# Attention layer of a four-layer decoder trunk: the last eight query and gate pieces laid evenly over softmax steps 18 to 28, the first output parts over steps 28 to 31

## The reference, cut to what matters

```
x <- x + RMSNorm_post(mixer(RMSNorm_pre(x)))
```

```
z = h @ w_in                    # 1024 -> q (16 heads x 64), k, v (2 heads x 64), g (1024)
q, k = rope(q), rope(k)
scores = q k^T / 8              # blocks of 128 queries against 256 keys
p = softmax over the keys, with one more "sink" term per head
o = p v
out = (o * silu(g)) @ w_out
```

## Time and profile before

| | us |
|---|---|
| median of 3 runs | 2237.68 (2237.27 to 2237.75) |
| the profiled execution | 2237.23 |
| its span, first to last instruction | 2235.3 |
| PE busy | 2197.0 (98%) |
| DVE busy | 1516.0 (68%) |
| ACT busy | 1118.0 (50%) |
| POOL busy | 107.0 (5%) |

### The profile page before, as it was taken

How to read it: one execution, slowest core, us unless ns; L and a number is a source line. 1 busy time by engine, 2 the same in 40 slices (tenths; PEclk the granted TensorE clock), 3 DMA queues, 4 the chain that set the end, 5 groups by cost and what they waited for, 6 DMA issues and landing times.

```text
span 2235.3 us, 40229 instructions
## 1 busy us (share of the span) xinstructions
PE 2197.0 (98%) x16495; PEld 2118.9 (95%) x16495; DVE 1516.0 (68%) x2211; ACT 1118.0 (50%) x1721; POOL 107.0 (5%) x101
## 2 busy tenths in 40 slices
PE   8999999999999999998999999999999999999997
PEld 7999999999999898887999999999999999999997
DVE  5987787787334756667367778368887787876245
ACT  7445555555332535456362476365546555555232
POOL 0000000000000014445000000000000000000000
PEclk9999999999999999999999999999999999999999
DMA  4322223234411431111322111324222222225213
GB/s 145 124 105 95 96 77 106 85 105 167 149 47 57 164 100 39 48 49 39 114 89 76 48 48 48 124 82 150 95 101 91 86 93 98 86 86 218 95 49 114
DMA packets 76535, 211.67 MB, mean 95 GB/s; under 512 B 10920, under 2 KB 31544, under 8 KB 76344
## 3 DMA queue, kind: packets, MB, share of 16 engines
q1 hardware_dynamic: 72944, 204.19, 26.6%
q10 hardware_dynamic: 3408, 4.90, 0.8%
HBM read 154.23 MB, written 51.13 MB: 92 GB/s over the span
## 4 chain that ended last, share of the span: by engine, by line
issue 43%; PE 42%; DVE 5%; POOL 3%; POOLq 2%; DVEq 2%; ACTq 1%; ACT 1%; DMA 0%
PE ps L1007 18%; PE ps L782 13%; PE ps L808 5%; POOL l_sc L763 3%; PE ps L868 2%; POOLq L762 2%; PE ps L951 1%; PE ps L1236 1%; PE ps L1136 1%; ACTq L1790 1%; POOLq L760 0%; PE ps L942 0%; ACTq L1765 0%; DVE l_hs L2619 0%; DVE l_rc L2608 0%
## 5 line engine op out<-in xcount | busy, mean ns | idle before, releaser
L1007 PE MATMUL ps<-l_h_hi,l_op_hi 128*128 128x258 f32 x1344 | 384.5, 286 | 0.7 <-DVEq L2158 0.7
L1007 PE MATMUL ps<-l_h_lo,l_op_hi 128*128 128x258 f32 x1344 | 379.3, 282 | 0.0
L1007 PE MATMUL ps<-l_t_hi,l_op_hi 128*128 128x258 f32 x1008 | 288.0, 286 | 3.2 <-ACT l_partial L1460 1.7
L1007 PE MATMUL ps<-l_t_lo,l_op_hi 128*128 128x258 f32 x1008 | 285.7, 283 | 0.0
L1007 PE MATMUL ps<-l_h_hi,l_pair_lo 128*128 128x258 f32 x1008 | 284.7, 282 | 0.0
L782 PE MATMUL ps<-l_y_lo,w_hi 128*128 128x344 f32 x816 | 260.0, 319 | 0.0
L1007 PEld LDWEIGHTS ps<-l_h_hi,l_op_hi 128*128 128x128 f32 x1344 | 254.3, 189 | 1.8 <-issue 1.1
L1007 PEld LDWEIGHTS ps<-l_h_lo,l_op_hi 128*128 128x128 f32 x1344 | 254.1, 189 | 0.0
L782 PE MATMUL ps<-l_y_hi,w_hi 128*128 128x344 f32 x726 | 232.5, 320 | 0.9 <-DVEq L2633 0.9
L782 PE MATMUL ps<-l_y_hi,w_lo 128*128 128x344 f32 x726 | 231.4, 319 | 0.0
L1846 DVE TENSOR_TENSOR w_lo<-w_raw,w_hi 128x1024 fp32r<-128x1024 f32 x97 | 122.1, 1260 | 147.0 <-ACT w_hi L1269 143.1
(11 more groups left out here) (314 smaller groups left out, 5520.8 us busy)
## 6 DMA issues: line engine op xcount, KB each, us to landing
w_raw<-in_wu SPq DMA_DIRECT2D x97, 512.0 KB, 3.4
l_pair<-in_wu SPq DMA_DIRECT2D x84, 512.0 KB, 3.5
l_vstage<-v_save SPq DMA_DIRECT2D x32, 516.0 KB, 3.9
y_save<-l_vstage SPq DMA_DIRECT2D x30, 516.0 KB, 2.6
l_y<-y_save SPq DMA_DIRECT2D x30, 516.0 KB, 10.6
v_save<-l_late_v SPq DMA_DIRECT2D x24, 516.0 KB, 2.7
x_save<-x SPq DMA_DIRECT2D x9, 1376.0 KB, 5.8
x<-x_save SPq DMA_DIRECT2D x21, 516.0 KB, 6.9
```

The lines of the kernel that those rows point to most:

```text
L1007: mm = nc.tensor.matmul(ps[:, 2 * j + ch, 0:QW], low[:, k, :] if t == 1 else L.op_hi[i][:, k, :], lo[:, k, :] if t == 2 else hi[:, k, :], ...
```

## The change

The table of pieces and the places of the output parts are written anew. Nothing is added or removed: the same 24 matmuls per piece and the same output parts of 3 matmuls per k-step.

```diff
-                       18: ((28, 0, HALF),), 19: ((28, HALF, KT), (29, 0, KT)), 20: ((30, 0, HALF),), 21: ((30, HALF, KT), (31, 0, KT)),
-                       22: ((32, 0, HALF),), 23: ((32, HALF, KT),), 24: ((33, 0, KT), (34, 0, HALF)), 25: ((34, HALF, KT),), 26: ((35, 0, KT),)}
+                       18: ((28, 0, 6),), 19: ((28, 6, KT), (29, 0, HALF)), 20: ((29, HALF, KT), (30, 0, 2)), 21: ((30, 2, KT),),
+                       22: ((31, 0, 6),), 23: ((31, 6, KT), (32, 0, HALF)), 24: ((32, HALF, KT), (33, 0, 2)), 25: ((33, 2, KT),),
+                       26: ((34, 0, 6),), 27: ((34, 6, KT), (35, 0, HALF)), 28: ((35, HALF, KT),)}
...
-                    if i == 27:
+                    if i == 28:
                         pe.wait_ge(w_lo_done, weighed(u + 18))
+                        pe.wait_ge(*L.piece_read.at(35))
+                        pe.wait_ge(*L.Lo.at(19))
+                        out_part(0, 0, range(0, 2))
+                    if i == 29:
+                        out_part(0, 0, range(2, 6))
+                    if i == 30:
                         pe.wait_ge(*L.piece_read.at(36))
-                        pe.wait_ge(*L.Lo.at(19))
-                        out_part(0, 0, range(0, 3))
-                    if i == 28:
-                        out_part(0, 0, range(3, 6))
-                    if i == 29:
                         pe.wait_ge(*L.Lo.at(22))
-                        out_part(0, 1, range(0, 3))
-                    if i == 30:
-                        out_part(0, 1, range(3, 6))
+                        out_part(0, 1, range(0, 4))
+                    if i == 31:
+                        out_part(0, 1, range(4, 6))
```

## The result

| us | before | changed |
|---|---|---|
| median, 22 runs each | 2237.72 (2236.6 to 2240.24) | 2241.95 (2239.67 to 2246.1) |
| ratio, 95% interval | | 1.0019 (1.0013 to 1.0024) |
| span of the profiled execution | 2235.3 | 2239.8 |

The changed kernel is slower by 4.2 us. That it is slower is certain, since the interval lies above 1. Whether it is slower by more than 0.2% is not, since the interval holds that border. Forecast were 2242.5 us and a rise of 4.8. The profiles show one execution each; the 22 executions of the changed kernel differ by 6.4 us.

The account below looks back on a forecast made before the run. PE, busy 98% of the span, was taken to bound the kernel. Waits +3.0, beginnings 0.3 and clock 1.5 made +4.8 us on 2237.23, plus 0.45 for the median: 2242.5 us, range 2237.6 to 2246.2.

Parts of the forecast that it names:

- before `scores(21)`: Steps 18 and 19: PE waits for maxima(20), which DVE begins later, 2.7 us, bounds 1.0 to 3.0.
- before piece 31 and `scores(24)`: Steps 21 and 22: PE waits 5.7 us for DVE's rotation of tile 7, 0.5 of them before piece 31.
- steps 26 and 27: PE has 9 matmuls less before values(26), the chain loses one tanh: waits 2.3 instead of 3.2 us.
- beginnings: On PE, 17 stretches of pieces and outputs become 19, costing 0.3 us.
- clock behind the first gap: Half clock on PE behind the 2.7 us wait before scores(21): 1.5 us, bounds 0 and 2.0.
- clock behind the second gap: Half clock on PE in step 22, behind the wait before scores(24): 2.0 us.
- clock in step 27: The 2.0 us lost to half clock in step 27 go, since 12 matmuls fill it.
- The stall: DVE's second or third rotation operation stretched to about 2 us beside POOL's multiply, which was taken not to move.
- The third rival: Only the gap of step 22 costs clock: +3.3 us, 2241.0 us, chance 0.17.
- The even spread does what its form says: Rival over the changed steps: all waits and the lost clock go, -10.1, 2227.6 us, chance 0.05.
- Further behind: Rival: both DVE stalls at the upper end, sample keys wait for the cache, +7.8, 2245.5 us, chance 0.08.
- DVE gets through in time: Rival in turns 21 and 22: POOL's multiply misses tile 7's rotation, wait 4.0; sum +0.6, 2238.3 us, chance 0.20.

Follow-up runs that it names:

- Experiment 3: Changed kernel without the nine vector operations that rotate query tile 7, waits and signals kept: 2234.78 us, ratio 0.9985 to the kernel before.
- experiment 1: Changed kernel with only its early part (steps 18 to 22); later pieces from step 24 and output parts as before: 2246.93 us, ratio 1.0039 to the kernel before.
- experiment 4: Changed kernel without POOL's last softmax multiply for blocks 19 and 22: 2236.25 us, ratio 0.9994 to the kernel before.
- Experiment 5: Changed kernel plus 16 and 30 unread matmuls in front of scores(21) and scores(24): 2239.21 us, ratio 1.0007 to the kernel before.
- experiments 2 to 6: Number 2, otherwise unnamed: kernel before up to step 25, piece 35 cut over steps 26 and 27, output parts over 28 to 31; 2237.04 us, ratio 0.9996.
- experiment 6: Against the changed kernel: unit 15 ends in step 19 as before, later pieces spread evenly over steps 20 to 27, output parts over 28 to 31; 2238.61 us.
- experiment 7: Against the changed kernel: table with 42 matmuls in step 19, 36 in step 21, fewer in others, piece 35 whole in step 27; 2233.41 us.

## Why the prediction was right

Step by step, as the prediction put them:

| step | forecast | measured |
|---|---|---|
| before `scores(21)` | 2.7 | 2.85 |
| step 20 | 0 | 0 |
| before piece 31 and `scores(24)` | 5.7 | 0.44 + 5.33 = 5.77 |
| steps 26 and 27 | 2.3 | 1.53 + 0.34 = 1.87 |
| before `values(30)` | 0.7 | 0.68 |
| before `turns(31)` | none | 0.54 |
| waits in all, before 8.44 | 11.4 | 11.71 |
| beginnings | 0.3 | none to be seen |
| clock behind the first gap | 1.5 | 1.49 |
| clock behind the second gap | 2.0 | 1.83 |
| clock in step 27 | -2.0 | -2.0 |
| span | +4.8 | +4.5 |

By the border of 2242.2 us that the prediction had drawn, the measured 2241.95 lies on the side of "same", which had 0.41, and not on that of "slower", which had 0.52. The rise is real but a little smaller than the forecast one. That the sum came so near is in part luck: the waits were 0.3 us larger than forecast, and the beginnings and the second fall smaller by 0.3 and 0.2.

*The large terms.* The method was to count both sides of a meeting from one common start, DVE's queue by distances of starts and PE's by matmuls. It gave 5.7 against 5.77. Experiment 3 shows that it is the rotation in turn 22, and experiment 1 that the loss comes from the early steps and not from the late ones.

*The stall.* The size was right (1.7 us, shown by experiment 4), the operation was not: the rows of before let me expect the second or third of the rotation, and it was the first in both places (982.27 and 1003.92). The multiply starts 0.05 us ahead of it each time. The premise that it doesn't move was wrong. It started at 982.77 before and at 982.22 now. By the rows, that is because POOL's small operation ahead of it ran before DVE's weights began (981.13) and not beside them (980.12). The first row is of before, the second of the changed kernel:

```profile
980.48 0.92 POOL L759 TENSOR_TENSOR l_rq<-l_mx 128x4 f32<-128x4 f32 x1 [6.99 <-ACTq L1696]
```

```profile
980.55 0.20 POOL L760 TENSOR_TENSOR l_rq<-l_mx 128x4 f32<-128x4 f32 x1 [6.99 <-ACTq L1698]
```

Both times now the multiply starts 1.09 us behind the start of the weights (981.13 and 1002.78). For the first gap I had counted a stall of 1.4 us instead of 1.66; it was 1.71, so DVE was 0.3 us later than forecast. PE was 0.15 us later as well (at 986.25 instead of 986.1), and the gap came out 0.15 us longer. The rival of a multiply that misses the rotation did not come; where the multiply would have had to start for that, no run tells.

*The clock.* That it falls behind a gap of 2.7 us was a choice between 0 and 2.0. It fell, at 1.49; that the chosen 1.5 met it so closely is luck. Experiment 5 confirms the sum of both. The third rival (only the second gap costs clock, +3.3 us) is refuted for the profiled execution by the window at 990, and the profiles of experiments 1 and 3 show the fall there too (0.64 and 0.58 in the window 990 to 994). For the 22 executions it isn't settled that each had both falls: their mean granted clock lies between 0.994 and 0.997, the three with 0.997 took 2239.9 to 2240.2 us and the two with 0.994 took 2244.0 and 2244.2.

*The late steps.* The 2.3 came out as 1.87. From `values(24)` to `values(26)` are 12.55 us before (1026.30 to 1038.85) and 11.70 now (1031.50 to 1043.20). So the chain became 0.85 us shorter and not 0.37 (the one tanh), and PE's own work fell by 1.20 and not 1.45: the wait is 1.53 and not 2.3. Against that, 0.34 stayed before `scores(29)`, where none was forecast. What else shortened the chain no run tells. The wait before `turns(31)` was missed. `turns(31)` hangs on a chain through `maxima`, `exps` and POOL that ran inside the 2.30 us of before. In the changed kernel that chain is longer, too. Two rows of the changed kernel belong to it, a small operation of POOL in step 31 and, in the second fence, the weights on DVE:

```profile
1065.47 0.91 POOL L760 TENSOR_TENSOR l_rq<-l_mx 128x4 f32<-128x4 f32 x1 [2.34 <-ACTq L1698]
```

```profile
1065.11 1.22 DVE L1848 TENSOR_TENSOR w_lo<-w_raw,w_hi 128x1024 fp32r<-128x1024 f32 x1
```

The operation of 128 x 4 took 0.91 us and ended at 1066.38, with the weights of DVE, which ended at 1066.33. In experiment 1, where step 31 is as before, it took 0.43 us. That the 0.48 us between them make the wait of 0.54 was not shown. The other profiles fit: in experiments 2 to 6 the operation took 0.90 to 0.92 us and `turns(31)` waited 0.53 to 0.55, and before and in experiment 1 it took 0.44 and 0.43 and nothing waited. But the last two also have the 2.30 us before `values(30)`, so that the two causes are not parted.

*The beginnings.* The 0.3 us for two more stretches were not seen. By the table of the change there are even three more, 17 become 20, which would make 0.45. Waits and clock alone give 4.6 us against 4.5 of span, so that nothing is left for them; a beginning of a stretch seems to cost less than the 0.15 us of the earlier trace rows, but no run took it apart.

*The rivals on the other side.* "The even spread does what its form says" is refuted by the result, and experiment 6 shows no gain from it even with unit 15 on time: an even load on PE did not help where its partner's load was uneven. "Further behind" is refuted by the waits: only two of DVE's turns were late by much, and the sample steps had 0.34 us. "DVE gets through in time" is refuted by the 5.33 us before `scores(24)`.

## What to carry to other kernels

Where one engine's list is laid against a second engine's, don't spread the work evenly but put the most of it beside the second engine's long turns: here the table with 42 and 36 matmuls beside the rotations was 8.5 us faster than the even one, with waits of 2.0 instead of 8.6 us in these steps. When a table moves the end of a unit by one step, count what hangs on that end (readout, weights, rotation) from a common start to its reader, on both engines; that gave the largest term within 0.1 us. And price a gap on the matrix engine with what the clock takes behind it, here 1.5 and 1.8 us more for gaps of 2.85 and 5.33 us.

## What was not expected of the hardware

- One gap of 2.85 us with full work on both sides was enough for half clock behind it, and cost 1.49 us. A gap of 2.28 us before `scores(23)` (experiment 6) was enough too: `scores(23)` took 2.08 us where 1.13 is the full-clock row. The gap of 2.30 us before `values(30)` was not, as these windows of the kernel before show:

```profile
1060.00:1066.00 6.00, 3.63 (x48) 2.62 (x43) 4.13 (x10) 3.22 (x11) 3.34 (x3) 1.00 0.01 3
1066.00:1084.00 18.00, 18.00 (x116) 17.21 (x115) 2.99 (x6) 5.91 (x10) 0.00 (x0) 1.00 0.69 265
```

- In experiment 7 the clock fell behind gaps of only 0.29 and 0.89 us, while PE was busy for 5.89 of 6 us (0.75 in the window 1046 to 1052). So the length of the gap alone does not decide. The Trainium skill (TensorE: Matmul & The Clock Gate, "What's actually happening") says of the start of a kernel that the moment at which the clock changes varies from run to run. No run here shows the moments in more than one execution; that the mean clock of the changed kernel lies between 0.994 and 0.997 fits it.
- 46 matmuls without any use made the kernel 2.7 us faster (experiment 5).
- What stands between DVE and POOL works the other way round too: an operation of 128 x 4 on POOL took 0.91 us and ended with DVE's weights beside it. In experiment 1, where it began 0.5 us later in their course, it took 0.43, and at 980.55 us in the changed kernel, ahead of the weights, 0.20.
